# First norm of a conditioned trunk layer: modulation summed in four channel chunks, with 24 projection units issued between the loads, and the last norm split over two engines

## The reference

```
mod = silu(c) @ w_ada + b_ada                 # w_ada is 2048 x 12288
sh1, sc1, g1, sh2, sc2, g2 = split(mod, 6)    # 2048 channels each
h = rms_norm(x, norm1_w) * (1 + sc1) + sh1
proj = h @ w_in                               # 2048 x 7168: q, k, v of attention; q, f, i, g of the recurrence
y = concat(dilated_window_attention, hgrn2) @ w_out
x = x + g1 * y
h = rms_norm(x, norm2_w) * (1 + sc2) + sh2
x = x + g2 * ((silu(gate) * up) @ w_down)     # gate, up: causal depthwise conv of h @ w_up
out = rms_norm(x, final_norm_w)
```

## Time and profile before

| | |
|---|---|
| runs | 1360.27, 1362.35, 1370.89 us |
| the profiled execution's own time | 1362.31 us |
| its span, first to last instruction | 1360.3 us |
| PE busy | 1229.8 us (90%) |
| DVE busy | 1023.1 us (75%) |
| ACT busy | 594.2 us (44%) |
| mean granted TensorE clock | 0.964 of full |
| DMA | 329.72 MB, mean 242 GB/s |

### The profile page before, as it was taken

One profiled execution on the slowest core, in us unless ns is written; L12 is line 12 of the kernel. 1 busy time (PEld: TensorE's weight loads), 2 busy tenths in 40 slices (PEclk: granted clock), 3 DMA queues, 4 the chain that ended last, 5 costly groups with the idle time before them and its releaser, 6 DMA issues.

```text
span 1360.3 us, 20231 instructions
## 1 busy us (share of the span) xinstructions
PE 1229.8 (90%) x7009; PEld 1077.7 (79%) x7009; DVE 1023.1 (75%) x1262; ACT 594.2 (44%) x762; POOL 57.4 (4%) x103
## 2 busy tenths in 40 slices
PE   0108999999999999979999999999999999999995
PEld 0108999899998777768888888888888878888884
DVE  5997888878878788768878888897867765545543
ACT  2104444444545654455544444445444434333332
POOL 3000000012022000000000000000000000000000
PEclk9757999999999999989999999999999999999997
DMA  9894987777769879756777777777666675555562
GB/s 375 345 416 126 399 319 264 241 229 247 229 191 305 301 269 382 247 178 234 248 245 234 233 242 232 238 231 240 187 192 191 187 262 194 192 196 191 187 201 77
DMA packets 138624, 329.72 MB, mean 242 GB/s; under 512 B 10693, under 2 KB 11446, under 8 KB 133570
## 3 DMA queue, kind: packets, MB, share of 16 engines
q1 hardware_dynamic: 134592, 316.71, 69.4%
q0 software_dynamic: 3424, 10.00, 2.0%
q10 hardware_dynamic: 546, 2.20, 0.4%
HBM read 323.09 MB, written 4.19 MB: 241 GB/s over the span
## 4 chain that ended last, share of the span: by engine, by line
PE 86%; DVE 6%; DMA 3%; issue 2%; ACT 2%; ACTq 0%; DVEq 0%; SPq 0%
PE bank L1034 24%; PE bank L1036 12%; PE bank L1055 6%; PE bank L1056 6%; PE bank L1057 6%; PE bank L798 5%; PE bank L812 5%; PE bank L814 5%; PE bank L800 4%; PE bank L801 4%; PE bank L813 4%; DMA astart<-in_w_ada 3%; DVE acc L1125 1%; PE bank L831 1%; PE bank L846 1%
## 5 line engine op out<-in xcount | busy, mean ns | idle before, releaser
L1190 DVE TENSOR_TENSOR wlo<-wraw,whi 128x1024 fp32r<-128x1024 f32 x404 | 494.2, 1224 | 285.2 <-ACT whi L542 282.8
L542 ACT ACTIVATE whi<-wraw 128x1024 fp32r<-128x1024 f32 x408 | 432.0, 1060 | 616.1 <-PE bank L1036 246.5
L1034 PE MATMUL bank<-h,whi 128*128 128x512 f32 x1408 | 490.9, 395 | 2.7 <-issue 2.7
L1036 PE MATMUL bank<-h,wlo 128*128 128x256 f32 x1408 | 391.3, 278 | 0.0
L1034 PEld LDWEIGHTS bank<-h,whi 128*128 128x128 f32 x1408 | 265.4, 188 | 64.6 <-issue 2.9
L1036 PEld LDWEIGHTS bank<-h,wlo 128*128 128x128 f32 x1408 | 265.7, 189 | 0.0
L798 PE MATMUL bank<-h,whi 128*128 128x256 f32 x512 | 149.7, 292 | 4.9 <-DVE wlo L1190 4.4
L800 PE MATMUL bank<-h,whi 128*128 128x256 f32 x512 | 147.3, 288 | 0.0
L801 PE MATMUL bank<-h,wlo 128*128 128x256 f32 x512 | 147.2, 287 | 0.0
L1055 PE MATMUL bank<-whi,act_hi 128*128 128x512 f32 x352 | 137.0, 389 | 0.3 <-DVE evt L1404 0.3
L1056 PE MATMUL bank<-wlo,act_hi 128*128 128x512 f32 x352 | 136.9, 389 | 0.0
(11 more groups left out here) (214 smaller groups left out, 1224.4 us busy)
## 6 DMA issues: line engine op xcount, KB each, us to landing
wraw<-in_w_up SPq DMA_DIRECT2D x176, 512.0 KB, 4.4
araw<-in_w_ada SPq DMA_DIRECT2D x128, 512.0 KB, 5.1
wraw<-in_w_in SPq DMA_DIRECT2D x112, 512.0 KB, 4.2
wraw<-in_w_down SPq DMA_DIRECT2D x88, 512.0 KB, 4.1
astart<-in_w_ada SPq DMA_DIRECT2D x32, 1024.0 KB, 7.3
wraw<-in_w_out SPq DMA_DIRECT2D x32, 512.0 KB, 5.6
x<-in_x ACTq DMA_DIRECT2D x1, 2048.0 KB, 18.0
x<-in_x POOLq DMA_DIRECT2D x1, 2048.0 KB, 12.4
```

The source lines that it names most:

```text
L542: act.activation(whi[:, slot], wraw[:, slot], ACT.Copy).then_inc(s_hi, 1)
L1034: pe.matmul(out, whi[:, slot, k, cols], h[:, kk].rearrange("p a t -> p (a t)"), start=(kk == 0), stop=False, skip_group_check=True)
L1036: last = pe.matmul(out[:, 0:SEQ], wlo[:, slot, k, cols], h[:, kk, 0, :], start=False, stop=(kk == KT - 1), skip_group_check=True)
L1190: dve.tensor_tensor(wlo[:, slot], wraw[:, slot], whi[:, slot].bitcast(F32), ALU.subtract).then_inc(s_lo, 1)
```

## The change

**Chunks.** The shift and scale of the first norm are summed for 512 channels at a time. A piece is now 128 rows x (512 shift columns + 512 scale columns), 512 KB in rows of 2 KB, in a ring of 12 (`pc`). There are four chunks of 16 pieces. DVE sums most pieces into `acc_c`. PE sums the others by itself: five in the first chunk (rows 1, 4, 7, 10, 13), three in each of the others (3, 7, 11), 14 in all, by using the piece as the weights and silu(c) as a one-column operand (8 matmuls a piece). `chunk_columns` then adds the partition sums of `acc_c` in the same bank (8 matmuls). The bias `b_ada` comes in through the transposed parameter rows.

**Units under the loads.** The first 24 units (three groups) run chunk by chunk: six units per chunk, two of each group, into banks 2, 0 and 4. While chunk c's units run, the pieces of chunk c + 1 are loaded and summed. On PE, `chunk_columns(c + 1)` stands after the fourth unit of chunk c, so the fifth and sixth come after it.

**x.** It is transposed unscaled; 1/rms goes into `rrow`, a row that multiplies each tile.

**Order of the modulations.** Gate 1, shift 2, scale 2. Four of the 96 pieces stand before step 24, where 21 stood; the output projection has 25 where it had 19. Gate 1 is now summed as columns, and turned into a row by diagonal matrices (`gate_diagonals`, 16 ACT copies; `gate_rows`, 4 matmuls). `out_columns` stands at steps 120, 128 and 136 (122, 129 and 137 before). `column_sums` runs six times, where it ran four times and `row_sums` twice.

**Before the second norm.** The hi and lo parts of unit 147 are moved behind `out_columns(3)`.

**Split tail.** Squares of the last norm are taken quarter by quarter in the down projection, the final weight is multiplied in there for three quarters, a square root ahead of time loads ACT's table, and the last scaling is split: four blocks on DVE and two on ACT, of 512 or 768 columns, six stores.

The core of the diff (semaphore declarations, memory offsets and renamed counters are left out):

```diff
+EARLY = 3
+CHUNKS, CT = 4, 4
+PER_CHUNK = 2 * EARLY
+EARLY_UNITS = CHUNKS * PER_CHUNK
...
+PC_RING = 12
+PE_TILES = ((1, 4, 7, 10, 13), (3, 7, 11), (3, 7, 11), (3, 7, 11))
...
-HALVES = ((SH2, 0), (SH2, 1), (SC2, 0), (SC2, 1), (G1, 0), (G1, 1))
+HALVES = ((G1, 0), (G1, 1), (SH2, 0), (SH2, 1), (SC2, 0), (SC2, 1))
 def piece_steps():
-    at = [3 + k for k in range(5)] + [8 + k for k in range(16)]
-    for n in range(3, 11):
-        at += [8 * n + k for k in ((1, 3, 4, 6, 7) if n < 6 else (1, 4, 6, 7))]
+    at = [EARLY_UNITS - 4 + k for k in range(4)]
+    for n in range(3, 9):
+        at += [8 * n + k for k in (1, 3, 4, 5, 6, 7)]
+    for n in range(9, 11):
+        at += [8 * n + k for k in (1, 3, 4, 6, 7)]
     for n in range(11, 14):
         at += [8 * n + k for k in (0, 1, 2, 3, 4, 5, 6)]
-    return at + [OUT0 + k for k in range(19)]
+    return at + [OUT0 + k for k in range(25)]
...
-OUT_AT = (OUT0 + 10, OUT0 + 17, OUT0 + 25)
-SUM_AT = (PIECE_AT[15] + 2, PIECE_AT[31] + 2, 76, 101, 118, 133)
+OUT_AT = (OUT0 + 8, OUT0 + 16, OUT0 + 24)
+SUM_AT = (PIECE_AT[15] + 3, PIECE_AT[31] + 3, 95, 108, 126, 140)
...
+FINAL_DVE = ((0, slice(0, 768)), (0, slice(768, 1536)), (0, slice(1536, D)), (1, slice(1536, D)))
+FINAL_ACT = ((1, slice(0, 768)), (1, slice(768, 1536)))
 class Phase:
...
-            with sp.Fori(0, KT // 2) as r:
-                for n, (mod, row) in enumerate(((SH1, 0), (SC1, 0), (SH1, 1), (SC1, 1))):
-                    sp.wait_ge(s_ada, r * 4 + (n + 1))
-                    sp.dma_start(astart[:, n], w_ada[bass.ds(r * (2 * P) + row * P, P), mod * D:(mod + 1) * D]).then_inc(s_as[n], 16)
+            def load_first(i):
+                if i >= PC_RING:
+                    if i - PC_RING in PC_OF_PE:
+                        sp.wait_ge(s_pcp, PC_OF_PE.index(i - PC_RING) + 1)
+                    else:
+                        sp.wait_ge(s_pcd, PC_OF_DVE.index(i - PC_RING) + 1)
+                ch, row = i // KT * CT * P, i % KT * P
+                src = w_ada[row:row + P, 0:2 * D].rearrange("p (m n) -> p m n", m=2)[:, :, ch:ch + CT * P]
+                sp.dma_start(pc[:, i % PC_RING], src).then_inc(s_pc[i % PC_RING], 16)
...
+            for r in range(KT):
+                load_first(r)
+                if r in (11, 13):
+                    load_in((r - 11) // 2)
+            load_in(2)
+            load_in(3)
+            for c in range(CHUNKS - 1):
+                for r in range(KT):
+                    load_first((c + 1) * KT + r)
+                    if r % 4 == 3:
+                        load_in(PER_CHUNK * c + RING + r // 4)
+                load_in(PER_CHUNK * c + RING + 4)
+                load_in(PER_CHUNK * c + RING + 5)
...
+            for n in range(CHUNKS - 1):
+                u0 = PER_CHUNK * n + RING
+                for j in range(4):
+                    first_hi(u0 + j)
+                chunk_hi(n + 1)
+                first_hi(u0 + 4)
+                first_hi(u0 + 5)
...
+            final_squares(3)
+            act.wait_ge(s_xsum, 1)
+            act.activation(rstd, ss, ACT.Sqrt, bias=epsc, scale=1.0 / D).then_inc(s_rt, 1)
+            act.wait_ge(s_rs, 1)
+            for n, (b, cols) in enumerate(FINAL_ACT):
+                act.activation(xr[:, b, cols], xr[:, b, cols], ACT.Copy, scale=ss[:, b:b + 1]).then_inc(s_fina, 1)
+                act.wait_ge(s_fina, n + 1)
+                act.dma_start(out_tok[:, b, cols], xr[:, b, cols]).then_inc(s_out, 16)
...
+                for k in range(2 * CT):
+                    last = pe.matmul(ps[6 + c % 2][:, k:k + 1], pc[:, i % PC_RING, k // CT, k % CT * P:(k % CT + 1) * P],
+                                     csilu[:, r:r + 1], start=(r == PE_TILES[c][0] and k == 0), stop=False,
+                                     skip_group_check=True)
+                last.then_inc(s_pcp, 1)
+            def chunk_columns(c):
+                pe.wait_ge(s_pcd, sum(i < (c + 1) * KT for i in PC_OF_DVE))
+                for k in range(2 * CT):
+                    last = pe.matmul(ps[6 + c % 2][:, k:k + 1], acc_c[:, c % 2, k * P:(k + 1) * P], ones[:, 0:1],
+                                     start=False, stop=True, skip_group_check=True)
                 last.then_inc(s_red, 1)
-            pe.wait_ge(s_ada, 2 * KT + 4)
...
+            for r in PE_TILES[0]:
+                first_piece(r)
+                if r == 4:
+                    for b in range(TB):
+                        pe.wait_ge(s_diag0, b + 1)
+                        last = pe.matmul(ps[7][:, b * P:(b + 1) * P], ones[:], diag0[:, b], start=True, stop=True)
+                    last.then_inc(s_row, 1)
+                elif r == 7:
+                    pe.wait_ge(s_in, 7 * 16)
+                    pe.wait_ge(s_prm, 2)
+                    for t in range(4):
+                        last = pe.transpose(ps[0][:, 97 + 88 * t:97 + 88 * (t + 1)], rows[0:88, 1 + t, :], ident[0:88, 0:88])
+                    last.then_inc(s_prmT, 1)
...
+                pe.wait_ge(s_lo, u + 1)
+                if n < EARLY:
+                    pe.wait_ge(s_h, UK * (j + 1))
+                if GROUPS[n][0] in ("hi", "av", "hg"):
+                    token_unit(BANK[n], j, u % RING, lambda kk, tok: h[:, kk, 0, tok], lambda kk, tok: h[:, kk, 1, tok], j * UK)
+                else:
+                    channel_unit(n, j, u % RING)
+                if u < EARLY_UNITS - PER_CHUNK:
+                    c, t = u // PER_CHUNK + 1, u % PER_CHUNK
+                    if t < 3:
+                        first_piece(c * KT + PE_TILES[c][t])
+                    elif t == 3:
+                        chunk_columns(c)
+                after(u)
...
+                for k in range(CT * c, CT * c + CT + 1):
+                    if k < CT * c + CT:
+                        if k >= 2:
+                            dve.wait_ge(s_h, k - 1)
+                        dve.scalar_tensor_tensor(out=htmp0[:, k % 2], in0=xT[:, k, :], scalar=A1[:, k:k + 1], in1=rrow[:],
+                                                 op0=ALU.mult, op1=ALU.mult).then_inc(s_ht, 1)
+                    if k > CT * c:
+                        dve.wait_ge(s_hhi, k)
+                        dve.scalar_tensor_tensor(out=h[:, k - 1, 1, :], in0=htmp0[:, (k - 1) % 2], scalar=B1[:, k - 1:k],
+                                                 in1=h[:, k - 1, 0, :].bitcast(F32), op0=ALU.add, op1=ALU.subtract).then_inc(s_h, 1)
...
+            for c in range(CHUNKS - 1):
+                v = PER_CHUNK * c + RING
+                for r in range(KT):
+                    if r not in PE_TILES[c + 1]:
+                        first_piece((c + 1) * KT + r)
+                    if r % 4 == 3:
+                        lo_part(v + r // 4 + 1, (v + r // 4) % RING, v + r // 4 - RING + 1)
+                chunk(c + 1)
+                for e in (4, 5):
+                    lo_part(v + e + 1, (v + e) % RING, v + e - RING + 1)
...
+                if k == 5:
+                    v = UP0 - 1 + AHEAD
+                    lo_part(v + 1, v % RING, UP0)
```

471 lines of the change are left out of this document (269 added, 202 removed).

## The result

The changed kernel takes 1357.32 us (median of 18 runs, 1348.60 to 1363.20), the kernel before 1362.45 (18 runs, 1360.27 to 1371.99). The ratio is 0.9939, with a 95% interval of 0.9915 to 0.9963: a gain of 0.6%, inside the 1% that I had called no change. I had forecast 1337, with a range up to 1358 that just holds it, and given "faster by over 1%" a chance of 0.80.

The account below looks back on a forecast made before the run. PE idles behind the loads and sums at first, then PE itself bounds the kernel after unit 24. Terms: -23.6 - 5.2 - 1.9 + 3.7 + 2.0 = -25.0 on span 1360.3 gives 1335.3; with 2.0 more, 1337 us; range 1319 to 1358.

Parts of the forecast that it names:

- Head: Start of the kernel up to unit 0: x, first-chunk pieces and column sums done so that unit 0 starts at 54.
- Period: Time per chunk under the loads: 19.2 pieces and remainders, 2.8 column sums, 7.1 added wait, 2.4 hi part and remainder; 31.5 us.
- the rival of half clock throughout: Under the loads, PE stays at half clock among one-column matmuls: 54 us later, 1391 us; chance 0.04.
- the sum with half clock at each turn: Chunk-to-chunk turns before unit 24, each paying for half clock in full: unit 24 at 168.6; 160.8 if full, 167 taken.
- The third, fourth and fifth term: Earlier work before the second norm gains 1.9; added PE work loses 3.7; moved pieces lose 2.0 in PE waits.
- Column sums: Added PE work: column_sums runs six times, not four, 2 x 1.85 = 3.7 us lost on PE's path.
- the first term: Stretch up to unit 24: it starts at 167 instead of 190.6, gain 23.6 us, bounds 3 and 40.
- Before the second norm: DVE's last columns no longer wait behind unit 147's parts: gain 1.9 us, bounds 0 and 2.5.
- The moved pieces: 17 pieces moved behind step 24 cost 2.0 us of PE waits at attention and transposes, bounds 0 and 20.4.
- The end: After the last addition: scaling starts at 1347.6, stores end at 1355.1; gain 5.2 us, bounds 3.5 and 6.5.
- Loads bound it: Before unit 24, pieces in 2 KB rows move at 307 GB/s: unit 24 at 188, 1358 us; chance 0.10.
- DVE or DMA bound after unit 24: After unit 24, moved pieces come back as PE waits, 20.4 in place of 2: 1355.7 us; chance 0.09.

Follow-up runs that it names:

- Two accumulators: The changed kernel with two accumulators per chunk written in turn, so no DVE piece waits for the sum just ahead; 1362.18 us, ratio 0.9954.
- remainders later: The changed kernel with the remainders of units 5 and 6 moved behind the next chunk's second and third piece; 1346.99 us, ratio 0.9853.
- thin dummies: The changed kernel with 24 unused one-column matmuls ahead of each column sum of chunks two to four; 1360.89 us, ratio 0.9947.
- wide dummies: The changed kernel with 24 unused 512-column matmuls ahead of each column sum of chunks two to four; 1343.88 us, ratio 0.9829.
- dummies there: The changed kernel with 12 unused 512-column matmuls at step 95, where PE waits for the softmax; 1354.05 us, ratio 0.9878.
- gates later: The changed kernel with the gate's diagonals and row matmuls at steps 116 to 122 instead of 90 to 102; 1351.77 us, ratio 0.9879.
- old end: The changed kernel with only its new ending (split last norm, scaling and stores) taken back; 1363.91 us, ratio 0.9958.

## Why the prediction was wrong

Up to unit 24 the mechanisms were the ones foreseen, and their sizes too small. Behind it, two things that cost several us stood in the sum at nothing.

**Head: right.** Unit 0 at 53.68 for 54; the next chunk's first piece at 57.85, for 59.5.

**Period: the step that failed.** I had 31.5 us from column sums to column sums; it was 34.5 (112.64 less 78.14). Three sizes went wrong.
- The pieces: 19.2 forecast, 20.3 measured from the first piece's start (92.35) to PE's sums. I took the distance from a piece to an independent subtraction for that from a piece to a piece which needs its sum. The same row says that a piece lasts 1.28, and here a dependent one starts only after its end: 1.39, at eight places in a chunk (remainders stand between the others), 1.5 us, less 0.35 for the first, a plain multiply. Two accumulators gave the 1.20 back.
- The sums: 2.8 forecast, 3.6 measured. I took a mean of the two clocks; it was half at all turns.
- The wait for the two token units and the remainders: 9.5 forecast, 10.65 measured (81.7 to 92.35). I had PE idle for 3 to 4 us before the sums; it was 5.8 to 6.0. And I gave 3.4 us of half clock by the gap of 4.42; the window 110 to 118 has 0.58 and the next six us 0.70, together some 10 us. The row was the nearest, but dense units followed it in that trace, while here 3.6 us of one-column sums follow the gap. The length of the gap alone doesn't explain it: with the remainders later, the third turn's gap was 4.18, shorter than 4.42, and the clock over 143 to 153 was 0.50. That the sums behind the gap make the difference is the reading that fits, with the thin dummies; no run put dense units behind such a gap.

I had noted this very thing as evidence for the rival of half clock throughout (chance 0.04), and then charged it nowhere in the forecast. In truth it was no rival but a part of each turn: wide dummies gave back 10.5 us. The Trainium skill ("TensorE: Matmul & The Clock Gate", HAM oscillation) says that such gaps bring the half clock back every time. The trace agrees, three turns of three. Even the sum with half clock at each turn, 168.6, was 7 too early: besides the pieces, I had priced a turn by the nearest gap and not by what follows it.

Step by step: the column sums stood at 78.14, 112.64 and 146.97 where my sum has 78.7, 110.2 and 141.7, and unit 24 at 175.44 for 168.6. That is 6.8 of the 8.4 us by which unit 24 is late; the other 1.6 are my step from 168.6 down to 167, toward a full clock that didn't come.

**The third, fourth and fifth term: 10.6 us lost where 3.8 were forecast** between unit 24 and the up projection. By stretches, against before: 1.5 gained up to unit 88, 8.8 lost in units 88 to 95, 3.2 in units 96 to 103, 0.1 from there on.
- Column sums: three more calls behind unit 24 than before (6 instead of 3), not two. One of the four earlier calls stood ahead of unit 24, in a stretch that the first term already counted. 5.6 instead of 3.7, at the full clock.
- The half clock at 432: nothing was charged. With dummies there the phase was 3.5 shorter, but that these did it is not shown (above). Before, the clock fell once in this phase, near 394, for 3.4 us; the change doesn't have that fall, which fits the 1.5 gained.
- The gates' rows and waits of PE: units 88 to 95 took 35.2 us, 26.4 before. In them are the sums at 3.4, two gates' rows (2.1, which before stood later), and waits of 4.3 against 1.3. I had put the gates' rows at nothing and the diagonals as covered, since ACT was 44% busy; a share over the whole says nothing of the steps in which ACT makes a softmax, the diagonals, and copies. The run with the gates later shows it: without them units 88 to 95 took 28.8, so 6.4 of the 8.8 are theirs. Moving them gained only 2.2 in all, since the rows take their time on PE at any place and met a second wait.
- Before the second norm: right, even larger. From the end of unit 143 to the up projection 7.9 us, before 11.0: 3.1 for 1.9. No run takes this edit back alone, and the half clock there was shorter too.
- The moved pieces cost nothing that can be seen: PE nowhere waits for `piece`.

**The end:** 4.8 for 5.2, shown by itself with the old end.

**The rivals.** Loads bound it: no, 386 GB/s at share 1.05 with rows of 2 KB alone, not 307. DVE or DMA bound after unit 24: no. The clock at half throughout: no, full between the turns.

**The rest of the miss**, 5.3 us between the profiled execution and the median, goes by all that is known to the spacing of the up projection. The run 1370.89 among the three of before was a sign of it that I passed over. Profile against profile, the change is worth 10.2 us; the lower groups of both kernels (medians 1361.65 and 1352.04) say 9.6.
